# First MoBA layer: second query and key slots as seven block products each, ahead of the softmax steps

## The reference

```python
proj = x @ w_in                      # (256, 1024) @ (1024, 3072)
q, k, v = jnp.split(proj, 3, axis=-1)
...
s = q @ k.T * 64 ** -0.5 + bias      # per head, causal
o = softmax(s) @ v
x = layer_norm(ALPHA * x + o @ w_out, g, b)
x = layer_norm(ALPHA * x + grouped_moe(x), g, b)
```

## Time and profile before

| what | value |
|---|---|
| time, median of 3 runs | 1199.26 us |
| time of the profiled execution | 1198.84 us |
| its span | 1197.1 us |
| PE busy | 1015.0 us (85%) |
| PE weight loads busy | 564.2 us (47%) |
| DVE busy | 340.4 us (28%) |
| ACT busy | 185.0 us (15%) |
| mean granted PE clock | 0.926 |
| DMA | 449.08 MB, mean 375 GB/s |

### The profile page before, as it was taken

How to read it: one execution, slowest core, us unless ns; L and a number is a source line. 1 busy time by engine, 2 the same in 40 slices (tenths; PEclk the granted TensorE clock), 3 DMA queues, 4 the chain that set the end, 5 groups by cost and what they waited for, 6 DMA issues and landing times.

```text
span 1197.1 us, 18620 instructions
## 1 busy us (share of the span) xinstructions
PE 1015.0 (85%) x7736; PEld 564.2 (47%) x7736; DVE 340.4 (28%) x912; ACT 185.0 (15%) x474; POOL 43.0 (4%) x109
## 2 busy tenths in 40 slices
PE   9999999976688976678999999999966889756766
PEld 7585544443343432243698655444533433433422
DVE  4535521321111111111563785303211111111112
ACT  1024210110010000000321563110100010100002
POOL 1001010000000000000100120100000000000000
PEclk9999999997799987788999999999987899888888
DMA  9937899999999999999993609999999999999995
GB/s 353 369 141 264 332 391 418 427 426 427 428 427 429 428 427 426 428 426 423 379 363 131 242 2 358 383 418 424 425 428 427 428 427 428 428 426 428 426 425 222
DMA packets 59349, 449.08 MB, mean 375 GB/s; under 512 B 4579, under 2 KB 10980, under 8 KB 32636
## 3 DMA queue, kind: packets, MB, share of 16 engines
q1 hardware_dynamic: 57248, 442.52, 90.0%
q0 software_dynamic: 1680, 4.88, 1.1%
q10 hardware_dynamic: 332, 0.42, 0.1%
HBM read 446.72 MB, written 1.07 MB: 374 GB/s over the span
## 4 chain that ended last, share of the span: by engine, by line
PE 54%; DMA 40%; DVE 3%; ACT 1%; issue 1%; SPq 1%; DVEq 0%
PE bank L1150 16%; DMA ring<-in_moe_w_gate 13%; DMA ring<-in_moe_w_up 11%; DMA ring<-in_moe_w_down 11%; DMA bias<-in_moe_w_up 5%; PE bank L1003 5%; PE bank L1114 4%; PE bank L932 4%; PE bank L903 4%; PE bank L1235 3%; PE bank L1211 2%; PE bank L1399 2%; PE bank L1250 2%; PE bank L1497 1%; PE bank L1222 1%; PE bank L1426 1%
## 5 line engine op out<-in xcount | busy, mean ns | idle before, releaser
L1150 PE MATMUL bank<-ring,work 128*32 128x256 f32 (+1 forms) x2656 | 334.9, 490 | 111.5 <-DMA ring<-in_moe_w_up 37.5
L1150 PEld LDWEIGHTS bank<-ring,work 128*32 128x32 f32 (+1 forms) x2656 | 154.0, 136 | 246.3 <-issue 217.2
L1867 DVE TENSOR_TENSOR work<-work,bank 128x256 f32<-128x256 f32 (+1 forms) x32 | 15.6, 488 | 521.2 <-PE bank L1150 521.2
L1150 PE MATMUL bank<-softmax_area,work 128*32 128x256 f32 (+1 forms) x352 | 67.2, 513 | 36.8 <-DMA ring<-in_moe_w_gate 26.5
L1235 PE MATMUL bank<-ring,work 128*32 128x512 f32 x576 | 87.7, 595 | 6.8 <-DMA ring<-in_moe_w_down 3.4
L1880 DVE TENSOR_TENSOR xs<-xs,bank 128x512 f32<-128x512 f32 x112 | 71.1, 683 | 41.5 <-PE bank L1253 23.3
L1150 PE MATMUL bank<-bias,work 128*32 128x256 f32 (+1 forms) x384 | 78.3, 495 | 0.0
L1114 PE MATMUL bank<-work,acc 128*128 128x128 f32 (+1 forms) x448 | 75.5, 323 | 0.0
L1114 PEld LDWEIGHTS bank<-work,acc 128*128 128x128 f32 x448 | 66.0, 191 | 16.6 <-issue 11.5
L1150 PEld LDWEIGHTS bank<-softmax_area,work 128*32 128x32 f32 (+1 forms) x352 | 31.6, 143 | 71.0 <-issue 65.7
L2282 ACT COPY work<-bank 128x256 f32<-128x256 f32 (+1 forms) x32 | 13.6, 425 | 326.4 <-PE bank L1187 257.1
(11 more groups left out here) (311 smaller groups left out, 1229.5 us busy)
## 6 DMA issues: line engine op xcount, KB each, us to landing
ring<-in_moe_w_gate SPq DMA_DIRECT2D x44, 2048.0 KB, 30.1
ring<-in_moe_w_up SPq DMA_DIRECT2D x40, 2048.0 KB, 28.8
ring<-in_moe_w_down SPq DMA_DIRECT2D x36, 2048.0 KB, 28.9
softmax_area<-in_moe_w_down SPq DMA_DIRECT2D x8, 2048.0 KB, 25.8
ring<-in_moe_w_down SPq DMA_DIRECT2D x12, 1024.0 KB, 8.1
ring<-in_moe_w_gate SPq DMA_DIRECT2D x12, 1024.0 KB, 8.9
bias<-in_moe_w_gate SPq DMA_DIRECT2D x6, 2048.0 KB, 34.4
softmax_area<-in_moe_w_up SPq DMA_DIRECT2D x6, 2048.0 KB, 28.7
```

The source lines that it names most:

```text
L1150: last = mm(bank[2 + k][row:row + cap, 0:width], xgT_of(group_of[i])[:, t, at + e * cap:at + (e + 1) * cap], w[e](t)[:, part * width:(part ...
```

## The change

The second query slot and the second key slot become two more units, "q1" and "k1", of seven block products each. All fourteen products stand ahead of `attention`; the first four steps of `beside` are now empty. Each unit uses two banks: p1 and p2 share bank 0, p6 and p7 bank 1, p5 and p3 bank 0 again, p4 bank 1, and a reader of the first of two waits until the second is written. PE begins q1 when all seven adds of the values are done. Pair 4 and the output projection wait for the last add of k1. The weight slots 4 and 5 come free when the unit's p4 is done. DVE makes q1's four weight sums after the router's centring, and k1's t3, t1 and t2 between the adds of the values; t4 of k1 goes behind q1's adds. Two of the input sums and the distance rows move to other places, to make room. Several semaphores that had one copy per layer become one, with counts that go on through the second layer.

```diff
+        SHARED_BANKS = {u: {"p1": "p2", "p6": "p7", "p5": "p3"} for u in ("q1", "k1")}
+        def unit_at(u, p):
+            return 2 * P * (u in SHARED_BANKS and p in SHARED_BANKS[u].values())
+        def written(u, p):
+            return products_through(u, SHARED_BANKS[u].get(p, p) if u in SHARED_BANKS else p)
...
+        MOBA_UNITS = {"k0": 1, "q1": 4, "k1": 5}
+        for u, before in (("q1", {}), ("k1", {"p1": ("q1", "p3"), "p6": ("q1", "p4")})):
+            unit_banks[u] = {"p1": (0, before.get("p1")), "p2": (0, None), "p6": (1, before.get("p6")), "p7": (1, None),
+                             "p5": (0, (u, "p2")), "p3": (0, None), "p4": (1, (u, "p7"))}
...
-        for n, g in ((0, 2), (4, 4), (5, 6)):
-            fixed_freed[0][n] = (proj_ready[0], g)
+        fixed_freed[0][0] = (proj_ready[0], 2)
+        for u, n in MOBA_UNITS.items():
+            fixed_freed[0][n] = (product_done, products_through(u, "p4"))
...
-        beside = [{0: [("proj", 4)], 1: [("proj", 5)], 2: [("proj", 6)], 3: [("proj", 7)],
+        beside = [{
                    5: [("out", 0)], 6: [("out", 1)], 7: [("out", 2)], 8: [("out", 3)], 9: [("out", 4)], 10: [("out", 5)]},
...
-                    pe.wait_ge(proj_dve[0], 3)
-                    pe.wait_ge(proj_act[0], 3)
+                    pe.wait_ge(product_added, adds_through("k1", "c21"))
...
+            def moba_products(k):
+                u, names = k
+                if u == "q1" and names == FOUR:
+                    pe.wait_ge(v_added, 7)
+                if names == FOUR:
+                    arrived(0, MOBA_UNITS[u])
+                unit_products(u, *names)
+            for u in ("q1", "k1"):
+                for names in (FOUR, THREE):
+                    moba_products((u, names))
             attention(0, moba_job, moba_products)
...
                 add(c21, c22, 4, 1)
+                weights_arrived(5)
+                sum_w_blocks("k1", "t3")
                 dve.wait_ge(v_psum, 3)
                 add(c12, c22, 0, 1)
+                sum_w_blocks("k1", "t1", "t2")
...
             centre_router(0, 7)
+            dve.wait_ge(dist_stored, 16)
+            weights_arrived(4)
+            sum_w_blocks("q1", "t3", "t1", "t2", "t4")
             add_values()
             dve.wait_ge(bias_loaded, 16)
+            add_products("q1", *ADDS_BEHIND[FOUR])
+            add_products("q1", *ADDS_BEHIND[THREE])
+            sum_w_blocks("k1", "t4")
+            add_products("k1", *ADDS_BEHIND[FOUR])
+            add_products("k1", *ADDS_BEHIND[THREE])
             softmax_steps(0, None)
...
             copy_values()
+            for u in ("q1", "k1"):
+                copy_product(u)
             softmax_steps(0)
```

More of the change, by code:

```diff
@@ L241, in unit_c @@
             at = slice(tt * P, (tt + 1) * P)
-            if u == "k0":
-                return kT[:, 2 * n:2 * n + 2, at]
+            if u in MOBA_UNITS:
+                first = (0 if u == "k0" else 4) + 2 * n
+                return (qT if u == "q1" else kT)[:, first:first + 2, at]
             if u == "kv":
@@ L891, in normed, with project_T @@
                 pe.wait_ge(normed_tiles, k)
-            def proj_bank_free(l, g):
-                after(pe, proj_dve[l] if g % 2 == 0 else proj_act[l], g // 2 - (l == 0))
-            def project_T(l, g, w, lhs_cols, free=False):
+            def project_T(g, w, lhs_cols):
                 b = g % 2
-                if not free:
-                    proj_bank_free(l, g)
                 for n, pick_cols in enumerate(lhs_cols):
@@ L929, in unit_products @@
                     w, x = unit_of[u][p]
+                    at = unit_at(u, p)
                     for n in range(2):
                         for t in range(HALF_K):
-                            last = mm(bank[b][:, n * P:(n + 1) * P], w[:, t, n * P:(n + 1) * P], x[:, t, :],
+                            last = mm(bank[b][:, at + n * P:at + (n + 1) * P], w[:, t, n * P:(n + 1) * P], x[:, t, :],
                                       start=(t == 0), stop=(t == HALF_K - 1))
@@ L1009, in out_piece @@
                     arrived(l, out_uses[l] + m // 4)
-                if m == 0:
-                    pe.wait_ge(proj_dve[l], (3, 3)[l])
-                    pe.wait_ge(proj_act[l], (3, 2)[l])
+                if m == 0 and l == 0:
+                    pe.wait_ge(product_added, adds_through("k1", "c21"))
+                elif m == 0:
+                    pe.wait_ge(proj_dve[1], 3)
+                    pe.wait_ge(proj_act[1], 2)
                 pe.wait_ge(o_copied[l], m + 1)
@@ L1174, in gate_up @@
                     keep_warm(1, b=3)
[L1175 removed]
+                block(1, range(KT)).then_inc(up_done, 1)
             def transpose_hidden(l, i):
[L1178 removed]
+                pe.wait_ge(hid_ready, PAIRS * l + i + 1)
                 after(pe, acc_added[l], 4 * (i - 2 if i < DOWN_FIRST else i - 1) + 1)
@@ L1492, in nsa_group @@
                     arrived(1, use)
-                    last = project_T(1, g, w, [tile_cols(0), tile_cols(1)], free=True)
+                    last = project_T(g, w, [tile_cols(0), tile_cols(1)])
                 else:
@@ L1864, in hidden @@
                     n = FF if i in WIDE_PAIRS else FF // 2
-                    dve.wait_ge(up_done[l], i + 1)
-                    dve.wait_ge(silu_ready[l], i + 1)
-                    v.tensor_tensor(hid[:, 0:n], silu[:, 0:n], bank[3][:, 0:n], ALU.mult).then_inc(hid_ready[l], 1)
+                    dve.wait_ge(up_done, PAIRS * l + i + 1)
+                    dve.wait_ge(silu_ready, PAIRS * l + i + 1)
+                    v.tensor_tensor(hid[:, 0:n], silu[:, 0:n], bank[3][:, 0:n], ALU.mult).then_inc(hid_ready, 1)
                 def add(i):
@@ L1897, in weigh @@
                         dve.wait_ge(ordered_ready, ordered_in(l) + 2 * i + 2 - FIXED)
-                    after(dve, pickwT_psum[l], i)
+                    after(dve, pickwT_psum, PAIRS * l + i)
                     dve.wait_ge(pick_ready[l], group_of[i] + 1)
@@ L1903, in weigh @@
                                                ws[:, :, 2 * i:2 * i + 2].unsqueeze(3).to_broadcast([P, NT, 2, cap]), ALU.mult)
-                    last.then_inc(pickw_ready[l], 1)
+                    last.then_inc(pickw_ready, 1)
                 def choose_next(i):
@@ L2219, in softmax_steps @@
                     for kind, k in beside[l].get(s, []):
-                        if kind == "proj" and k % 2 == 1:
-                            (moba_copy if l == 0 else nsa_copy)(k)
+                        if kind == "proj" and l == 0 and k[1] == FOUR:
+                            copy_product(k[0])
+                        elif kind == "proj" and l == 1 and k % 2 == 1:
+                            nsa_copy(k)
                     if s >= 2:
@@ L2274, in gated @@
                     n = FF if i in WIDE_PAIRS else FF // 2
-                    act.wait_ge(gate_done[l], i + 1)
-                    after(act, hid_ready[l], i)
-                    s_.activation(silu[:, 0:n], bank[2][:, 0:n], ACT.Silu).then_inc(silu_ready[l], 1)
+                    act.wait_ge(gate_done, PAIRS * l + i + 1)
+                    after(act, hid_ready, PAIRS * l + i)
+                    s_.activation(silu[:, 0:n], bank[2][:, 0:n], ACT.Silu).then_inc(silu_ready, 1)
                 def copy_hidT(i):
@@ L2290, in copy_pickwT @@
                 def copy_pickwT(i):
-                    act.wait_ge(pickwT_psum[l], i + 1)
+                    act.wait_ge(pickwT_psum, PAIRS * l + i + 1)
                     if i > 1:
                         act.wait_ge(spread_ready[l], 4 * i)
-                    s_.copy(picksT(i).rearrange("p t q -> p (t q)"), bank[3][:, 0:SEQ]).then_inc(pickwT_ready[l], 1)
+                    s_.copy(picksT(i).rearrange("p t q -> p (t q)"), bank[3][:, 0:SEQ]).then_inc(pickwT_ready, 1)
                 def copy_y(i):
```

117 lines of the change are left out of this document (56 added, 61 removed), and 4 rows, old and new, of tables (adds_through, products_through).

## The result

The kernel after takes 1205.55 us (median of 5 runs, 1204.96 to 1207.21), the kernel before 1199.89 in the same job (5 runs). The ratio over all runs is 1.0052, interval [1.004, 1.0064]; that of the medians is 1.0047, 5.66 us slower. The forecast was 1205.5, 6.25 us slower. The profiled execution took 1204.96 us with a span of 1203.2, so it is 6.12 us above the one of before.

What follows compares the result with a forecast made beforehand. PE's chain through the first layer's attention was taken as the bound: +0.86 - 3.4 + 7.9 = +5.35, plus 0.9 for the clock, +6.25 on 1198.84 gives 1205.1; the median, 0.42 higher, 1205.5 us. Range 1203.2 to 1208.6.

Steps and rivals of the forecast that it cites:

- A shift of the first layer's attention that runs through to the end: PE's chain releases all that follows the first layer's attention, so its full shift of 6.25 us reaches the end.
- Rival (d): The DMA stream, not PE, sets the layer and gains by earlier up weights: 1192.6 to 1199.3 us; chance 0.05.
- The wait: Ahead of the products: the first one waits for the seventh value add, so PE begins at 61.2, not 60.34: +0.86 us.
- The products: Ahead of attention: fourteen products run without holes in 25.0 us, replacing four groups of 28.4 us: -3.4 us.
- rival (e): The products don't close up; the add chain stalls PE at bank hand-overs: 1206 to 1207 us; chance 0.07.
- The bare steps: First layer's early softmax steps, without projections between them, follow their own latency: 8.0 us becomes 15.9, +7.9 us.
- Rival (b): Bare steps run at DVE's pace, ScalarE's copy not holding back the transposes: +4.05, 1203.3 us; chance 0.10.
- The clock: In the bare steps PE's granted clock falls after an idle gap, slowing matmuls: +0.9 us, bounds 0 and 7.
- (a): The clock holds through the bare steps: +5.35, 1204.6 us; chance 0.10.
- (c): The lower clock feeds itself and stays low until the output pieces: 1209.0 to 1211.6 us; chance 0.08.
- Mine is longer than the first, so I take a fall: PE's 3.6 us gap before job 2's scores exceeds an earlier 3.21 us gap with a clock fall, so it falls too.
- first long DMA piece near 244: Sign in the new profile: the chain of waits has its first long DMA piece near 244 us, before at 237.95.

Runs made afterwards that it cites:

- e6: Changed kernel, but the loads of expert pair 0's up weights wait for DVE's fourth read of scores, not the key slot's p4; 1206.11 us, ratio 1.0065.
- e4: Changed kernel, but the first product waits for six value adds, not seven; 1204.55 us, ratio 1.0044.
- e2: Kernel before, with its four plain projection groups and their copies moved ahead of the softmax steps, no products; 1207.09 us, ratio 1.0069.
- e1: Changed kernel, but the fourteen products, their adds and copies go back beside the first four softmax steps; 1196.31 us, ratio 0.9979.
- e7: Changed kernel with idle-filling matmuls, results unused, behind the scores of steps 0, 1 and 3; 1204.67 us, ratio 1.0044.
- e5: Changed kernel, but in the first layer DVE scales job 0 in step 1, behind the reads of job 1; 1203.84 us, ratio 1.0044.
- e8: Changed kernel, but in steps 2 to 4 of the first layer ACT copies transposed probabilities before the exponentials; 1204.40 us, ratio 1.0052.
- e9: Changed kernel with e4, e5 and e8 together, plus one idle-filling product of 512 columns behind the scores of steps 0, 1 and 3; 1201.36 us, ratio 1.0016.
- e3: Changed kernel with three idle-filling matmuls of 512 columns, results unused, between the scores of pairs 1 and 2; 1204.44 us, ratio 1.0043.

## Why the prediction was right

**What sets the time.** "A shift of the first layer's attention that runs through to the end" holds: the table's last two columns, and e6, which moves the loads and not the shift. Rival (d) is refuted.

**The terms.** Against the forecast of +0.86, -3.4, +7.9 and +0.9:

- The wait: A stood 0.11 ahead of V before, and the products start 0.75 behind it after. That is +0.86, and e4 gets 1.05 back when the wait goes.
- The products: 60.72 to 85.92 is 25.20, so -3.2 against 28.4. There are no holes; rival (e) is refuted, and the cover of the weight sums was right. "As seven products for eight blocks should be" was a coincidence, though: of the 3.2, 0.7 is four blocks closing up (e2) and only 2.5 the products' own saving (e1: 2.6), which is less than an eighth of 27.72. One instruction of 128 columns takes 1.79 / 16 = 0.112 us, one of 256 columns 27.72 / 128 = 0.217, so the narrow ones cost 3% more per column.
- The bare steps: S - A without the clock's share is 15.82 (e7), so +7.8. One reading was off without effect: the exponentials are 1.77 us ahead of the copy behind them (96.70 to 98.47 in the earlier trace rows), not 1.85. The links came as worked out: DVE reads at A + 0.98, 5.40, 8.33, 11.35 and 14.69, for 1.0, 5.5, 8.6, 11.5 and 15. e5 and e8 show the two orders that were named as what matters, at 1.8 and 0.6 us, each with the clock low over other steps than in after. At full clock the two together are worth 2.65 (15.82 in e7, 13.17 in e9).
- Rival (b) is refuted for the kernel after, where the transposes do wait for ACT's copy (0.84 and 0.52 us at 98.06 and 101.08). Its price was wrong too: three steps of 3.2 from 5.5 put the read of job 4 at 15.1, and PE's next scores wait 1.2 us more for DVE. That makes 16.3, not 14.6.
- The clock: 16.74 - 15.82 = 0.92. Rivals (a) and (c) are refuted for the kernel after: the clock did fall, and was back before the output pieces. e6's 10.2 us at the lower level is the way towards (c), and cost 1.2 us more than after's 6.8, far from 4.4.

The sum, 0.86 - 3.2 + 8.74 = 6.40, is the 6.39 of S - V. That the median came within 0.05 us of the 1205.5 is luck: the forecast started from 1199.26, the runs of before beside it had 1199.89, and the growth was 0.59 less than the 6.25. The profiled execution grew by 6.12, the medians by 5.66. V itself stands 0.48 earlier after than before; over the ten profiled kernels other than before it lies at 59.78 to 60.38, before at 60.45. Whether the edits ahead of V won 0.3 us or one execution of before was late there stays open.

**Where it was wrong without a price.** "Mine is longer than the first, so I take a fall": the gap of 3.48 us was to be the cause. e3 fills it and the fall comes later; e5 has no gap above 1.30 us and the clock falls; e7 and e9 fill all of them and it holds. The moments speak against the gap's length as well: in after the clock fell 1.15 us into the gap (89.08 to 92.56), in e2 0.84 us into its own, in e4 0.28 us behind it. That PE works thinly over the bare steps as a whole (6.05 of 9 us busy in e5, 8.20 in e7) fits the runs better, but how thin is too thin is not shown: e3, with 6.50 of the same 9, kept its clock there and lost it in the next steps.

The forecast of a fall was right by its outcome, for a reason that the runs don't bear out, and that the size met after's 0.92 is in part luck. S - A of e4, e3 and e6, which have its links, stands 0.50, 1.20 and 2.16 above e7's 15.82, so the price depends on where the fall begins and how long it lasts.

The Trainium skill's "TensorE: Matmul & The Clock Gate", section "Why this matters for your kernels", warns of long idle gaps between bursts. After and e2 have both such a gap (3.48 and 3.47 us) and a fall, but e5 shows that keeping the gaps short is not enough, and the measurement decides.

The mark "first long DMA piece near 244" was missed: it starts at 265.29. The chain stays on PE for a round longer; why it passes by the earlier wait I can't tell from the trace. The transfer that PE waited for behind the gap of 2.45 us before (it went on at 261.46) let it go on at 268.19 after. A switch of the chain from one engine to another is a poor mark; the start of an instruction behind it is a good one.

## What to carry to other kernels

Work that is independent of a chain of short steps on several engines is worth more between them than ahead of them: here 28 us of projections hid 8 us of latency, and a saving of 3 us in these projections became a loss of 6 by their place. Before moving such work, walk the steps bare, link by link with durations from the profile, and count the order in which each engine takes its operations. To compare kernels, find the first instruction behind the change from which all keep the same order, and one ahead of it: their distance (S - V) measured a term of 1.05 us (e4) that two overlapping intervals of the time did not show.

## What the runs showed of the hardware

- The clock fell with no idle gap above 1.30 us (e5) and 1.15 us into one of 3.48 (after), and a filled gap of 3.5 us put the fall off by 7 us rather than away (e3). Matmuls without use in every thin place held it (e7, e9); by themselves they bought 0.9 us (e7).
- A block product of 16 matmul instructions takes 1.79 us behind another and 0.1 more next to scores, on either side (e1), and four groups take 0.7 us less when they stand together (e2). Taking turns between kinds of matmul work is not free, here about 0.2 us a turn.
- The stretch at the lower clock lasted 3.4 us in e3 and e4, 6.8 in after, e2, e5 and e8, and 10.2 in e6, and with it kernels alike up to there came 0.5 to 2.2 us apart from e7 behind it.
